# One matrix per head for both directions of a chunked delta rule

## What is computed

```python
gc = jnp.cumsum(gc, axis=-1)
decay = jnp.exp(jnp.where(incl, gc[..., :, None] - gc[..., None, :], -jnp.inf))
kk = jnp.einsum('bhid,bhjd->bhij', kc, kc)
a = eye + jnp.where(strict, kk * decay * bc[..., :, None], 0.0)
rhs = jnp.concatenate([vc * bc[..., None], kc * (bc * jnp.exp(gc))[..., None]], axis=-1)
sol = lax.linalg.triangular_solve(a, rhs, left_side=True, lower=True, unit_diagonal=True)
u, w = sol[..., :dv], sol[..., dv:]
v_new = u - jnp.einsum('bhcd,bhde->bhce', w, S)
qk = jnp.where(incl, jnp.einsum('bhid,bhjd->bhij', qc, kc) * decay, 0.0)
o = (jnp.einsum('bhcd,bhde->bhce', qc * jnp.exp(gc)[..., None], S)
     + jnp.einsum('bhij,bhje->bhie', qk, v_new))
S = (S * jnp.exp(g_last)[..., None]
     + jnp.einsum('bhcd,bhce->bhde', kc * jnp.exp(g_last - gc)[..., None], v_new))
```

## Time and profile before

| | |
|---|---|
| median of 3 runs | 4572.24 us (4570.91 to 4575.46) |
| span of the profiled execution | 4540.2 us |
| delta-rule stage (first product to last norm) | about 842 us of it |
| PE, DVE, POOL, ACT busy in the span | 83%, 69%, 28%, 16% |

### The profile page before, as it was taken

The page is one execution under the profiler, slowest core; times in us unless marked ns, Lnnn a source line. Parts: engine busy times, 40 slices in busy tenths (PEclk is TensorE's granted clock), DMA queues, the critical chain, the costliest instruction groups (busy, mean ns, idle before and its releaser), DMA issues.

```text
span 4540.2 us, 42538 instructions
## 1 busy us (share of the span) xinstructions
PE 3783.4 (83%) x13554; PEld 2105.3 (46%) x13554; DVE 3120.7 (69%) x6438; ACT 734.0 (16%) x1805; POOL 1267.1 (28%) x1220
## 2 busy tenths in 40 slices
PE   7879889998989888897698987787789878777777
PEld 3334348643467777776654542232233247322222
DVE  3756537677667676664778758878876756788666
ACT  1231110024312221211100110010110021101000
POOL 0001100001033343330033333343354500335433
PEclk9889989999889999999899999999999999999999
DMA  5423235544200000004299999999999932899998
GB/s 212 176 102 142 81 130 195 213 166 160 89 5 24 6 26 6 24 6 197 81 394 401 363 374 421 401 401 412 397 416 404 422 157 75 364 413 401 419 421 364
DMA packets 140144, 1073.77 MB, mean 236 GB/s; under 512 B 15504, under 2 KB 15888, under 8 KB 21520
## 3 DMA queue, kind: packets, MB, share of 16 engines
q0 software_dynamic: 112608, 820.04, 44.4%
q1 hardware_dynamic: 27312, 251.02, 14.6%
HBM read 1060.51 MB, written 10.49 MB: 236 GB/s over the span
## 4 chain that ended last, share of the span: by engine, by line
PE 42%; DVE 35%; DMA 9%; issue 7%; POOL 4%; ACT 3%; DVEq 1%; POOLq 0%; SPq 0%; ACTq 0%
PE bank L199 20%; DVE arena L2909 11%; DMA arena<-in_uv,arena 6%; PE bank L2863 5%; DVE arena L2916 4%; POOL arena L2893 3%; PE bank L2423 2%; PE bank L2146 2%; DVE arena L443 2%; ACT arena L211 2%; DVE arena L221 2%; PE bank L2138 2%; DVE arena L217 2%; DVE arena L561 2%; PE bank L1620 2%
## 5 line engine op out<-in xcount | busy, mean ns | idle before, releaser
L2863 PE MATMUL bank<-arena 128*128 128x512 f32 x3072 | 1508.2, 621 | 403.1 <-DVE arena L2916 397.2
L199 PE MATMUL bank<-arena 128*128 128x128 f32 (+5 forms) x4896 | 1297.0, 424 | 77.7 <-ACT arena L211 36.9
L2893 POOL DMA_INDIRECT arena<-in_uv,arena x768 | 839.9, 1094 | 1297.2 <-PE bank L2863 631.9
L2863 PEld LDWEIGHTS bank<-arena 128*128 128x128 f32 x3072 | 541.2, 192 | 1343.3 <-DVE arena L2916 839.9
L2909 DVE CUSTOM_DVE_ANT_0 arena<-arena 128x1024 f32<-128x1024 f32 x768 | 941.8, 1226 | 278.2 <-DMA arena<-in_uv,arena 202.6
L199 PEld LDWEIGHTS bank<-arena 128*128 128x128 f32 (+3 forms) x4896 | 813.3, 195 | 550.3 <-issue 418.7
L211 ACT ACTIVATE arena<-arena 128x1 f32<-128x1 f32 (+6 forms) x1089 | 331.7, 305 | 2609.3 <-DVE arena L2909 1819.0
L211 ACT ACTIVATE arena<-bank 128x512 f32<-128x512 f32 (+3 forms) x464 | 248.2, 535 | 1060.8 <-PE bank L2125 491.0
L2916 DVE TENSOR_SCALAR arena<-arena 128x128 f32<-128x128 f32 x768 | 289.0, 376 | 173.1 <-ACT arena L211 113.1
L2208 POOL TENSOR_TENSOR arena<-arena 128x512 f32<-128x512 f32 x128 | 163.4, 1277 | 432.5 <-PE bank L2138 425.1
L443 DVE CUSTOM_DVE_ANT_0 arena<-arena 128x1024 f32<-128x1024 f32 x192 | 240.9, 1255 | 33.3 <-DMA arena<-in_w_rows 21.7
(11 more groups left out here) (251 smaller groups left out, 2836.8 us busy)
## 6 DMA issues: line engine op xcount, KB each, us to landing
arena<-in_w_rows SPq DMA_DIRECT2D x50, 1024.0 KB, 5.0
arena<-in_w_in SPq DMA_DIRECT2D x16, 2048.0 KB, 7.9
arena<-in_wq SPq DMA_DIRECT2D x14, 2048.0 KB, 8.2
arena<-in_dn_w SPq DMA_DIRECT2D x12, 2048.0 KB, 8.9
arena<-in_w_up SPq DMA_DIRECT2D x11, 2048.0 KB, 7.9
arena<-in_dn_wo SPq DMA_DIRECT2D x8, 2048.0 KB, 11.1
arena<-in_w_rows POOLq DMA_DIRECT2D x14, 1024.0 KB, 5.4
arena<-in_uv,arena POOLq DMA_INDIRECT x768, 10.7
```

The lines of the kernel that those rows point to most:

```text
L199: t = p.e.matmul(out, l, r, start=(i == 0), stop=(i == n - 1))
L2863: t = p.e.matmul(by[half], m["dg"][ee % 4], m["uv"][r][:, 1024 + 512 * half:1536 + 512 * half], start=(ee == 0), stop=(ee == 127))
L2893: g.e.indirect_dma_start(out=m["uv"][q % 7], out_offset=None, in_=self.I["uv"], in_offset=bass.IndirectOffsetOnAxis(ap=m["idx"][n % 2][:, ...
```

## The change

Both directions of one chunk become one **pair**, and all that is made ahead of the recurrence is made once per pair and not once per direction.

- Decays: the forward decay is at most 1 on one triangle and the backward one on the other, so min(forward, backward) before one exp gives both triangles in one square. One AT, one k·k and one k·q per chunk, one set of 8x8 blocks. The old PE outer products L1929 and L1935 go: DMAs with a broadcast source (`decay_rows`, from a new DRAM copy of the decay rows) write the decay rows into E and F (`sp_decay`), and those for the queries into Q (`sp_queries`).
- Beta no longer multiplies AT over 512 columns: `pe_beta`, `dve_beta`, `act_beta` make small tables once, BR for the 8x8 blocks and BS for the doublings.
- The inverse works on one matrix W that holds both triangles. A doubling is: transpose of W (PE), R = transpose times triangle mask (DVE), product with N (PE), T = that times BS (DVE), product with B, the masked W (PE; B is made by POOL), W minus that (DVE). After the last doubling POOL cuts the two triangles out of W (`in.XT`), and cuts the two triangles O out of E in a new part `stage`.
- The directions meet a pair at different times, so the recurrence runs two steps behind the inverse instead of one: 18 rounds of `chunks` instead of 17.

The core of the diff:

```diff
     def dve_decay(self, v, m, k, d):
+        V, c = self.V, k % 4
+        x, lo = (m["F"][k % 2] if d else m["E"][k % 4]), k // 4 * 4
+        v.wait_ge(*self.D.of(f"pg{d}{'ab'[k % 2]}.in", k))
+        v().tensor_tensor(heads(x, 4), heads(x, 4), bc(m["GC"][:, d, c, lo:lo + 4], 2, 128), ALU.subtract
+                          ).then_inc(*V.up("pr.d", k, d))
+        if d:
+            E = m["E"][k % 4]
+            v().tensor_tensor(E, E, x, ALU.min).then_inc(*V.up("pr.min", k))
...
+    INVERSE = 25
+    def pe_inverse(self, p, m, k):
+        P, V, G, W = self.P, self.V, self.G, m["W"][k % 2]
+        for r in range(self.INVERSE):
+            n, part = divmod(r, 6)
+            l = n + 3
+            if part == 0 and l < 7:
+                p.wait_ge(*V.of("in.W", k, l - 1))
+                b = self.banks.take(p, "in.tr", k, l)
+                for h in range(4):
+                    t = p.e.transpose(b[:, H4[h]], W[:, H4[h]], self.ident)
...
+            if part == 2:
+                p.wait_ge(*G.of("in.N", k, l))
+                p.wait_ge(*V.of("in.R", k, l))
...
+            if part == 4:
+                p.wait_ge(*V.of("in.T", k, l))
+                p.wait_ge(*G.of("in.B", k, l))
...
     def pool_inverse(self, g, m, k):
+        for r in range(self.INVERSE):
+            if r == 0:
+                g.wait_ge(*V.of("pr.A", k))
+                off(3)
+                tri(3)
+            if r in (3, 9, 15):
+                off(r // 6 + 4)
+            if r in (6, 12, 18):
+                tri(r // 6 + 3)
+            if r == 24:
+                g.wait_ge(*V.of("in.W", k, 6))
+                for d, sg in ((0, 1), (1, -1)):
+                    if k > 1:
+                        g.wait_ge(*P.of("re.vn", k - 2, d))
+                    self.pool_triangle(g, self.inverse_at(m, d, k), W, sg).then_inc(*G.up("in.XT", k, d))
...
-        for k in range(17):
-            paced(([((inverse or none)(e, m, k), 1)] if k < 16 else []) + ([((recur or none)(e, m, k - 1), 2)] if k else [])
-                  + ([(first(k + 1), 1)] if k < 15 else [])
+        for k in range(18):
+            paced(([(inverse(e, m, k), 1)] if k < 16 else []) + ([(recur(e, m, k - 2), 2)] if k > 1 else [])
+                  + ([(stage(e, m, k - 1), 1)] if 0 < k < 17 else [])
+                  + ([(prep(e, m, k + 1), 1)] if k < 15 else [])
```

More of the change, by code:

```diff
@@ L1720, in sp_dnproj @@
                 s.e.dma_start(self.xrest, self.x.rearrange("p t n -> p (t n)")).then_inc(*self.D.up("xrest.out", 0))
+        for d in range(2):
+            s.wait_ge(*self.V.of("ng.gx", d))
+            s.e.dma_start(self.crest[d], self.L["dn"]["gcr"][d]).then_inc(*self.D.up("crest.out", d))
     def np_acc(self, m, j):
@@ new lines, in sp_queries, with pe_beta @@
+    def sp_queries(self, s, m, k):
+        if k % 4 == 0:
+            return
+        for d in range(2):
+            if k > 1:
+                s.wait_ge(*self.P.of("re.o", k - 2, d))
+            s.e.dma_start(heads(m["Q"][d][k % 2], 4), self.decay_rows(d, k, self.chunk_of(d, k))
+                          ).then_inc(*self.D.up(f"pq{d}{'ab'[k % 2]}.in", k))
+    def pe_beta(self, p, m):
+        P, V, A = self.P, self.V, self.A
+        for d in range(2):
+            p.wait_ge(*V.of("bt.z", d))
+            b = self.banks.take(p, "bt.r", d)
+            p.e.matmul(b, m["block"], m["W"][d], start=True, stop=True).then_inc(*P.up("bt.r", d))
+            self.banks.give(("bt.r", d), A.of("bt.r", d))
@@ new lines, in dve_beta @@
+    def dve_beta(self, v, m):
+        V = self.V
+        v.wait_ge(*self.D.of("masks.in", 0))
+        for d in range(2):
+            be = m["BE"][:, d].rearrange("p t h -> p (t h)")
+            v().tensor_tensor(heads(m["W"][d], 64), bc(be, 2, 8), bc(m["start"][:, 4 * d, :], 1, 64), ALU.mult
+                              ).then_inc(*V.up("bt.z", d))
+        for l in range(4):
+            bs = m["BS"][:, l]
+            ts(v, bs, m["BE"][:, 0], m["side"][:, 0, l:l + 1], None, ALU.mult, None).then_inc(*V.up("bt.s0"))
+            v().scalar_tensor_tensor(bs, m["BE"][:, 1], m["side"][:, 1, l:l + 1], bs, ALU.mult, ALU.add
+                                     ).then_inc(*V.up("bt.s", l))
@@ new lines, in act_prep, with pool_prep @@
+    def act_prep(self, a, m, k):
+        E = m["E"][k % 4]
+        for r in range(self.PREP):
+            if r == 2:
+                a.wait_ge(*self.V.of("pr.min", k))
+                act(a, E, E, ACT.Exp).then_inc(*self.A.up("pr.e", k))
+            yield
+    def pool_prep(self, g_, m, k):
+        for r in range(self.PREP):
+            if r == 7:
+                g_.wait_ge(*self.D.of("masks.in", 0))
+                g_.wait_ge(*self.V.of("pr.A", k))
+                if k:
+                    g_.wait_ge(*self.P.of("in.ab", k - 1))
+                g_().tensor_tensor(heads(m["prod"], 4), heads(m["AT"][k % 2], 4), bc(m["block"], 1, 4), ALU.mult
+                                   ).then_inc(*self.G.up("in.prod", k))
+            yield
@@ new lines, in dve_prep @@
+    def dve_prep(self, v, m, k):
+        for r in range(self.PREP):
+            if r < 2:
+                self.dve_decay(v, m, k, r)
+            if r == 4:
+                E = m["E"][k % 4]
+                v.wait_ge(*self.A.of("pr.e", k))
+                ts(v, E, E, TINY, TINY, ALU.add, ALU.subtract).then_inc(*self.V.up("pr.cut", k))
+            if r in (5, 6):
+                self.dve_products(v, m, k, r - 5)
+            if r in (8, 9, 10):
+                self.dve_block(v, m, k, r - 8)
+            if r in (12, 13, 14, 15):
+                self.dve_substitute(v, m, k, r - 12)
@@ L2444, in sp_zsteps @@
     def sp_zsteps(self, s, m):
+        s.wait_ge(*self.D.of("xrest.out", 0))
+        for d in range(2):
+            s.wait_ge(*self.D.of("crest.out", d))
+        for k in range(2):
+            self.sp_decay(s, m, k)
         for k in range(16):
```

465 lines of the change are left out of this document (192 added, 273 removed).

## The result

| | before | after |
|---|---|---|
| median of 14 runs | 4571.35 us (4552.29 to 4583.07) | 4586.28 us (4578.99 to 4596.78) |
| span of the profiled execution | 4540.2 us | 4581.7 us |
| stage of the delta rule in it | 842 us | 879 us |
| the rest of that span | 3698 us | 3703 us |

The changed kernel is slower by 0.4%: 1.0042 times the kernel before, 95% interval 1.0028 to 1.0056, so clear of the noise though small. Forecast were 4543 us, 29 less than before; measured are 15 more. 4586 lies inside the range of 4480 to 4605, but on the other side of the kernel before. Four of the 14 runs of the kernel before took 4552 to 4559 us and the other ten 4568 to 4583.

A forecast was written before the change was run, and what follows sets the result against it. PE was taken to bound the stage, with some loss from two chains not fully covering each other. Steps walked at full clock sum to 768 us, plus 45 for clock: 813, 29 less than before, so 4543 us; range 4480 to 4605.

The forecast's parts named there:

- The base: Whole kernel: profiled span 4540.2 us, median of runs 32.0 us more; that difference was carried over unchanged.
- What goes: Work per step of the stage: PE left with 26.3 us, DVE with 30.1 us and then the busiest engine.
- The turn: After a pair's last W: V2 filled 6.05 us after PE's last product; DVE waits 4 to 5 us in ten steps.
- The plain step: Step with its recurrence on a group's second or third chunk: 51 us at full clock.
- The other steps: At full clock: first of a group 39 us, last 49, two without recurrence 26 and 27, last plain one without prep 41.
- The collision of DVE and POOL: DVE's decays and minimum beside POOL's work: 0 to 1 us a step, 0 to 16 in all, 0 in the sum.
- The clock: PE at 1.2 GHz after waits of about 3 us: 0 to 67 us over the stage, 45 taken.
- The lag of two: Behind the last pair, two recurrences with nothing beside them: 20.5 and 22 us.
- Decay rows by DMA: Broadcast DMAs of 256 KB, issued a step ahead, bounded by 2.4 to 10 us each: zero cost.
- Marks: Signs in the profile: stage about 813 us, clock 0.75 to 0.85, groups 195 to 205 us apart; wrong outside 45 to 60 us steps.
- the clock rival: All four doublings at 1.2 GHz: 146 us in all, 4644 us at worst; with the collision the slower side, chance 0.29.
- The rival of the busiest engine: Busiest engine sets the pace: step 38 us, stage 673, time 4403 us; chance 0.08 including anything under 4480.

The follow-up runs named there:

- e1_fill: Changed kernel with POOL's fill of V2 for the forward direction moved to the end of the recurrence ahead: 4531.43 us, ratio 0.9907.
- e4_rfirst: Changed kernel with DVE's first R of a pair written one round earlier, ahead of V2 and the forward decay: 4586.70 us, ratio 1.0027.
- e2_warm: Changed kernel with spare, overwritten PE products put where PE waits, to keep its clock up: 4552.27 us, ratio 0.9954.
- e9_early: Changed kernel with DVE's two decays and the minimum of a pair made a step earlier, where POOL is idle: 4573.78 us, ratio 0.9998.
- e10_best: As e7_turn, with spare PE products, overwritten by the real ones, at three of PE's waits: 4428.23 us, ratio 0.9678.
- e7_turn: Changed kernel with early V2 fill, recurrence and projection spread over the step, R first, early decays, N ahead of POOL's selects: 4455.76 us, ratio 0.9731.
- e3_spread: Changed kernel with only the written order changed: recurrence mostly every third round, projection every sixth instead of fourth: 4509.98 us, ratio 0.9856.

## Why the prediction was wrong, point by point

The forecast was 4540.2 - 842 + 813 + 32.0 = 4543 us. The measured terms are 4581.7 - 879 + 879 + 4.6 = 4586 us. The stage is 66 us longer than forecast, the rest of the span 5 longer, the difference to the median 27 smaller: 66 + 5 - 27 makes the 43 us (rounded). The step that failed is the walk's length for the steps other than the plain one, within the 768 us of the sum at full clock. With the clock kept up the stage took 838 us and not 768: 58 of these 70 us lie in those steps, 10 in the six plain ones, 2 at the edges. The clock gave back 41 us where the sum had 45; 70 - 4 are the 66.

- **The base (wrong, and it hid the miss).** "I carry the difference over unchanged." It came from one quick execution whose stage was 842 us where two others had 863 and 868. The error worked in favour of the forecast: from the typical base, its own stage of 813 us would have meant about 50 us less, and the miss of the stage would have stood bare. The range would have stood as much lower and would have ended below 4586: that it holds the result is luck.
- **What goes (right).** PE's full-clock work was put at 26.3 us a step, about 450 us in all, DVE's at 480. DVE is busy 453. PE is busy 565 at a mean clock of 0.81, and 565 x 0.81 is 457 (an estimate, since 0.81 is the mean of the stage and not of its busy time).
- **The turn (right).** V2 behind two selects, N, B and the fill: 6.1 us forecast, 6.2 measured. Waits of 4 to 5 us, ten or more: 63.7 us, 14 times, longest 5.8. e1_fill shows that they lie on the path. That R stands behind V2 was named too; e4_rfirst shows it to cost nothing by itself.
- **The plain step (right).** 51 us at full clock; in e2_warm, at a clock of 0.92, it has 52.7.
- **The other steps (the term that failed).** The first steps were put at 39 us and are 44.7, the last ones at 49 and are 57.2, the two without recurrence at 26 and 27 and are 33.2 and 32.0, the last plain one at 41 and is 51.9. Together they miss by 70 us at the real clock, and by 58 with the clock kept up (65.7 + 176.1 + 166.1 + 46.7 against 397). Per step with the clock kept up that is 5.0 us for a first one, 6.4 for a last one, 5.7 for the last plain one and some 6 for each of the two without recurrence. Three parts of it are known. Half clock: in these steps 12 sets of eight still took over 1.9 us in e2_warm, and the chain's products and transposes there are 17 us longer than at full clock, so that some 40 of the 58 us remain as the walk's own even if all of that is on the path. The collision of DVE and POOL, which the sum took as 0 within a range of 0 to 16: some 8 us by e9_early, and it falls on the first steps and on the second one without recurrence. The last steps of the changed kernel: DVE's operation L2338 waits there for PE's outputs (L199) 9.8 us a step, and 3.1 in a plain one, and V2 waits 7.3 us for the fill. What the walk had for these waits it doesn't say, so the rest of the cause stays open.
- **The clock (right in mechanism, and nearly in size).** Forecast: 6.2 us at most per plain step, 1 per first one, 45 in all, a clock of 0.75 to 0.85. Measured: 0.81, and e2_warm gives back 4.6 us per plain step and 41 in the stage. That is probably a lower bound, since its own clock is 0.92. The Trainium skill ("TensorE: Matmul & The Clock Gate", section "What's actually happening") calls throttled the default and activity what releases it; the granted clock agrees, since work that PE need not do raised it from 0.81 to 0.92.
- **The lag of two (right).** Two recurrences with nothing beside them: 42.5 us forecast, 44.6 measured.
- **Decay rows by DMA (right).** They are issued a step ahead; no wait of L2060 for a DMA appears in the stage.
- **Marks.** Groups were to lie 195 to 205 us apart; they lie 216.3 and 218.6 (the first norms, L2359, start at 1516.77, 1733.04 and 1951.60). The plain steps are within the 45 to 60 that was to show the prediction right, so that mark could not tell.

Of the rivals, the clock rival put the point at which the change turns against the kernel at 30 us above the sum and gave it, with the collision, 0.29. It is the nearest, but the excess was in neither: the clock cost 41 us or more (45 in the sum), the collision some 8 (0 in the sum), and steps walked short are the rest. The rival of the busiest engine (673 us) named what the order could give; e10_best, with the same work on DVE, comes to 723.

So why did a fifth of PE's and DVE's work in the stage bring nothing? Half of the chains went, and with them what one chain did in the waits of the other. What is left in program order is one chain of 21 us a step, a turn in which POOL's queue holds DVE, a crowded start of the step and an empty end of it, and PE's clock falls in those waits. The gain was there: 76 us lay in two numbers of pacing and 55 in one fill that stood in the wrong place.

## What to carry to other kernels

When a change halves the independent chains, it also halves what covers their round trips: place the fillers anew (here their pace, from 2 and 4 to 3 and 6) before judging it. Walk every kind of step as carefully as the commonest one; here the plain step was right to 4%, and the others were 5 to 6 us too short each even with the clock kept up. Before a single profile serves as the base of a sum, compare its span with the median: 32 us, where every other profile here is within 10, meant that the stage in question had been quick, and a second profile would have said so. And a mean clock over a stage says little: see which products of the chain are slow.

## What the runs showed of the hardware

- The same program's stage had granted clocks of 0.91, 0.88 and 0.89 in three executions, and took 842, 868 and 863 us. The changed one had 0.81 and 879 us twice.
- 336 product instructions more on PE made the changed kernel 34 us faster, and 192 more made e7_turn 27.5 us faster.
- In the changed kernel 51 of the chain's 128 sets of eight products took over 1.9 us, in e3_spread, with the same instructions in another order, 18.
- DVE operations with two SBUF inputs took 1.15 to 1.64 us beside POOL's selects and products and 0.69 without them (L2060 and L2064).
